# Fourier mixer with folded tokens: two transforms over 256 tokens in place of one over 512

## What is computed

```python
def fourier_mixer(h, w_in, w_out):
    B, N, _ = h.shape
    u, z = jnp.split(h @ w_in, 2, axis=-1)
    ug = u.astype(jnp.float32).reshape(B, N, FT_GROUPS, FT_GROUP_DIM)
    y = jnp.fft.fft2(ug, axes=(1, 3), norm='ortho').real.reshape(B, N, D_INNER)
    return (y.astype(h.dtype) * jax.nn.silu(z)) @ w_out
```

## Time and profile before

| what | value |
|---|---|
| median of 3 runs | 2701.87 us (2699.59 to 2704.38) |
| the profiled execution, its own time | 2705.14 us |
| span from its first to its last instruction | 2703.4 us |
| mean granted TensorE clock | 0.979 |
| TensorE matmul busy | 2556.3 us, 95% of the span |
| DVE busy, ACT busy | 1602.4 us (59%), 1003.5 us (37%) |
| Fourier mixer with its prologue and epilogue | about 1041 to 1315 us of the span |

### The profile page before, as it was taken

How to read it: one execution, slowest core, us unless ns; L and a number is a source line. 1 busy time by engine, 2 the same in 40 slices (tenths; PEclk the granted TensorE clock), 3 DMA queues, 4 the chain that set the end, 5 groups by cost and what they waited for, 6 DMA issues and landing times.

```text
span 2703.4 us, 40281 instructions
## 1 busy us (share of the span) xinstructions
PE 2556.3 (95%) x14516; PEld 2192.1 (81%) x14516; DVE 1602.4 (59%) x2276; ACT 1003.5 (37%) x1334; POOL 113.5 (4%) x140
## 2 busy tenths in 40 slices
PE   6999999999999998999899999989999899999996
PEld 1788888888888775888689999978988667888885
DVE  5567777777777744333455343468999755544445
ACT  3334443443354323333235222235445443322222
POOL 0011211111121000000000000000000000000000
PEclk9999999999999998999899999989999899999998
DMA  5122211222122222211122222222222212222222
GB/s 223 63 70 70 77 63 62 73 75 70 54 78 70 93 94 70 67 65 62 56 86 93 93 85 93 87 84 90 98 86 87 83 56 89 90 95 96 94 93 85
DMA packets 59816, 224.33 MB, mean 83 GB/s; under 512 B 6496, under 2 KB 6496, under 8 KB 59136
## 3 DMA queue, kind: packets, MB, share of 16 engines
q1 hardware_dynamic: 56544, 207.94, 22.8%
q0 software_dynamic: 3232, 15.86, 1.6%
HBM read 221.68 MB, written 2.10 MB: 83 GB/s over the span
## 4 chain that ended last, share of the span: by engine, by line
PE 85%; DVE 7%; ACT 4%; issue 3%; DMA 1%; DVEq 0%; ACTq 0%; SPq 0%; POOL 0%
PE ps L436 74%; PE ps L595 4%; PE ps L617 1%; PE ps L493 1%; DVE w_lo L1310 1%; DVE cv L1870 1%; ACT L934 1%; DMA ada_raw<-in_ada_weights_dram 1%; PE ps L636 1%; PE ps L608 1%; PE ps L627 1%; PE ps L582 1%; PE ps L629 1%; PE ps L628 1%; ACT w_hi L839 0%
## 5 line engine op out<-in xcount | busy, mean ns | idle before, releaser
L839 ACT ACTIVATE w_hi<-w_raw 128x1024 fp32r<-128x1024 f32 x360 | 381.4, 1060 | 1016.2 <-PE ps L436 1010.0
L1310 DVE TENSOR_TENSOR w_lo<-w_raw,w_hi 128x1024 fp32r<-128x1024 f32 x360 | 439.1, 1220 | 281.4 <-ACT w_hi L839 279.5
L436 PE MATMUL ps<-n_hi,w_hi 128*128 128x512 f32 (+1 forms) x992 | 324.0, 358 | 30.1 <-DVE w_lo L1310 16.4
L436 PE MATMUL ps<-n_hi,w_lo 128*128 128x512 f32 (+1 forms) x992 | 320.4, 355 | 0.0
L436 PE MATMUL ps<-n_lo,w_hi 128*128 128x512 f32 (+1 forms) x992 | 320.4, 355 | 0.0
L436 PE MATMUL ps<-h_hi,w_hi 128*128 128x512 f32 x640 | 273.7, 428 | 8.4 <-DVE h_lo L1337 4.4
L436 PE MATMUL ps<-h_hi,w_lo 128*128 128x512 f32 x640 | 255.3, 399 | 0.0
L436 PE MATMUL ps<-h_lo,w_hi 128*128 128x512 f32 x640 | 254.7, 398 | 0.0
L436 PEld LDWEIGHTS ps<-n_hi,w_hi 128*128 128x128 f32 x992 | 175.1, 190 | 66.4 <-issue 21.6
L436 PEld LDWEIGHTS ps<-n_lo,w_hi 128*128 128x128 f32 x992 | 176.3, 191 | 27.2 <-issue 0.2
L436 PEld LDWEIGHTS ps<-n_hi,w_lo 128*128 128x128 f32 x992 | 175.6, 190 | 26.6
(11 more groups left out here) (330 smaller groups left out, 5059.9 us busy)
## 6 DMA issues: line engine op xcount, KB each, us to landing
w_raw<-in_weights_dram SPq DMA_DIRECT2D x376, 512.0 KB, 3.3
ada_raw<-in_ada_weights_dram SPq DMA_DIRECT2D x4, 2048.0 KB, 25.9
gate_raw<-in_gate_weights_dram POOLq DMA_DIRECT2D x16, 512.0 KB, 3.6
x<-in_x_dram SPq DMA_DIRECT2D x1, 2048.0 KB, 11.8
x<-in_x_dram POOLq DMA_DIRECT2D x1, 2048.0 KB, 8.0
out_dram<-fin POOLq DMA_DIRECT2D x1, 2048.0 KB, 6.5
xc<-in_ctx_dram POOLq DMA_DIRECT2D x1, 1024.0 KB, 12.0
F_raw<-in_seq_dft_dram POOLq DMA_DIRECT2D x1, 1024.0 KB, 5.7
```

The source lines that it names most:

```text
L436: last = nc.tensor.matmul(o, w, xp, start=start and n == 0, stop=stop and n == 2)
L839: run(w_hi[:, s], w_raw[:, s], ACT.Copy).then_inc(hi_ready[s], 1)
L1310: tt(w_lo[:, s], w_raw[:, s], w_hi[:, s].bitcast(F32), ALU.subtract).then_inc(lo_ready[s], 1)
```

## The change

Tokens t and 512-t are folded. For t = 1 to 255 the cosine rows of t and 512-t are equal and the sine rows are opposite, so the cosine sums need only u[t] + u[512-t] and the sine sums only u[t] - u[512-t]. Token 0 stands for itself; token 256 is left out of the transform and added behind it as u[256] times +-1/sqrt(512), from a constant row `middle`.

- ACT no longer copies u whole. It copies the upper half of the bank (256 columns) to `u_up`, and DVE's new `fold(k)` writes the sums to `u_st[1:256]`, the differences to `u_st[257:512]` (in0 is PSUM, in1 is `u_up` read backwards) and tokens 0 and 256 to columns 0 and 256.
- `over_tokens(a)` keeps its 12 matmuls, but the six of token tiles 0 and 1 (the sums) run over the 258 first columns of `F` into bank 6 + a, the six of tiles 2 and 3 (the differences) over its 256 last columns into bank 4 + a. `F` holds 256 rows in place of 512.
- `p` is put together from three pieces: DVE adds the middle token to the cosines in `cosines(a)` (128x257, to `p_cos`), ACT copies the sines (128x255, from bank 4 + a) and then `p_cos` to `p_hi`, and DVE makes `p_lo` with two subtractions (`spectrum_lo`). `keep_middle` saves u[256] of both tiles (128x2).
- The semaphore `ft_acc` is parted: banks 0 and 1 are freed for z's projection by the fold (`u_folded`) and for u's by silu(z) (`z_out`).
- The table `F` that is loaded and cut before the loop is half as large; two memsets fill `middle`.

```diff
@@ pe_group
-                    pe.wait_ge(ft_acc, i * 4 + (k + 1))
+                    pe.wait_ge((z_out, u_folded)[k // 2], i * 2 + (k % 2 + 1))
...
-                    pe.wait_ge(ft_acc, j * 4 + 4)
+                    pe.wait_ge(u_folded, j * 2 + 2)
...
                     for t in range(TT):
-                        last = three([ps[:, 6 + a]], u_hi[:, a, tile(t)], u_lo[:, a, tile(t)],
-                                     [F_hi[:, t]], [F_lo[:, t]], t == 0, t == TT - 1)
+                        part, m_ = divmod(t, FOLD)
+                        o, c = ((ps[:, 6 + a, 0:BF], slice(0, BF)),
+                                (ps[:, 4 + a, 0:HALF_T], slice(HALF_T, T)))[part]
+                        last = three([o], u_hi[:, a, tile(t)], u_lo[:, a, tile(t)],
+                                     [F_hi[:, m_, c]], [F_lo[:, m_, c]], m_ == 0, m_ == FOLD - 1)
@@ act_group
+                    if k < 2:
+                        if j is not None:
+                            act.wait_ge(u_folded, i * 2 + (k - 1))
+                        run(u_up[:, k], ps[:, k, HALF_T:T], ACT.Copy).then_inc(up_copied, 1)
+                        return
...
+                def spectrum_hi(a):
+                    if j is not None:
+                        pe(2 + a)
+                        run(p_hi[:, a, HALF_T + 1:T], ps[:, 4 + a, 1:HALF_T], ACT.Copy)
+                        act.wait_ge(cos_done, j * 2 + (a + 1))
+                        run(p_hi[:, a, 0:HALF_T + 1], p_cos[:, a], ACT.Copy).then_inc(act_ft, 1)
...
-                hi(2, p_hi[:, 0], ps[:, 6])
-                hi(3, p_hi[:, 1], ps[:, 7])
+                spectrum_hi(0)
+                spectrum_hi(1)
@@ before dve_group
+            for n in range(2):
+                own.link(v.memset(middle[:, n:HALF_T + 1:2], (-1) ** n / T ** 0.5))
@@ dve_group
+                def fold(k):
...
+                    if j is not None:
+                        dve.wait_ge(pe_ft, j * 5 + 1)
+                    dve.wait_ge(up_copied, i * 2 + (k + 1))
+                    u, up, down = ps[:, k], ps[:, k, 1:HALF_T], u_up[:, k, HALF_T - 1:0:-1]
+                    tt(u_st[:, k, 1:HALF_T], up, down, ALU.add)
+                    tt(u_st[:, k, HALF_T + 1:T], up, down, ALU.subtract)
+                    v.tensor_copy(u_st[:, k, 0:T:HALF_T], u[:, 0:T:HALF_T]).then_inc(u_folded, 1)
...
+                def cosines(a):
...
+                        dve.wait_ge(pe_ft, j * 5 + (2 + a))
+                        stt(p_cos[:, a], middle[:], u_mid[:, a:a + 1], ps[:, 6 + a, 0:HALF_T + 1], ALU.mult, ALU.add
+                            ).then_inc(cos_done, 1)
...
+                def spectrum_lo(a):
...
+                        dve.wait_ge(act_ft, j * 8 + (3 + a))
+                        tt(p_lo[:, a, HALF_T + 1:T], ps[:, 4 + a, 1:HALF_T], p_hi[:, a, HALF_T + 1:T].bitcast(F32),
+                           ALU.subtract)
+                        tt(p_lo[:, a, 0:HALF_T + 1], p_cos[:, a], p_hi[:, a, 0:HALF_T + 1].bitcast(F32), ALU.subtract
+                           ).then_inc(dve_ft, 1)
...
                 next_block(0)
                 lo(1, u_lo[:, 0], ps[:, 4], u_hi[:, 0])
                 lo(2, u_lo[:, 1], ps[:, 5], u_hi[:, 1])
+                keep_middle()
+                fold(0)
                 next_block(1)
-                lo(3, p_lo[:, 0], ps[:, 6], p_hi[:, 0])
-                lo(4, p_lo[:, 1], ps[:, 7], p_hi[:, 1])
+                fold(1)
+                cosines(0)
+                spectrum_lo(0)
+                cosines(1)
+                spectrum_lo(1)
                 next_block(2)
```

More of the change, by code:

```diff
@@ L57 @@
 BF = 258
+HALF_T = T // 2
+FOLD = TT // 2
 _sizes = [("c", 2 * KD), ("ada_b0", 16), ("gate_b", 16), ("ada_b1", 16), ("norm_g0", KD), ("norm_g1", KD),
@@ L228, in program @@
         g_hi, g_lo = f.take("g_hi", [P, KD, T], F32R), f.take("g_lo", [P, KD, T], F32R)
-        F_hi = f.take("F_hi", [P, TT, T], F32R)
-        F_lo = f.take("F_lo", [P, TT, T], F32R)
+        F_hi = f.take("F_hi", [P, FOLD, T], F32R)
+        F_lo = f.take("F_lo", [P, FOLD, T], F32R)
         C_hi = f.take("C_hi", [P, 2, 2, 2, P], F32R)
@@ L240, in program @@
         raw = f.over()
-        F_raw, C_raw = raw.take("F_raw", [P, TT, T]), raw.take("C_raw", [P, 2, 2, 2, P])
+        F_raw, C_raw = raw.take("F_raw", [P, FOLD, T]), raw.take("C_raw", [P, 2, 2, 2, P])
         u_st, zf_st = f.take("u_st", [P, 2, T]), f.take("zf_st", [P, 2, T])
@@ L245, in program @@
         o_sb, yf, yg = f.take("o_sb", [P, 256]), f.take("yf", [P, T]), f.take("yg", [P, T])
+        middle, p_cos = f.take("middle", [P, HALF_T + 1]), f.take("p_cos", [P, 2, HALF_T + 1])
+        u_mid, u_up = f.take("u_mid", [P, 2]), f.take("u_up", [P, 2, HALF_T])
         b = g.over()
@@ L314, in program @@
         meta_scaled, meta_hi = sem("meta_scaled"), sem("meta_hi")
-        ft_acc, pe_ft, act_ft, dve_ft = sem("ft_acc"), sem("pe_ft"), sem("act_ft"), sem("dve_ft")
+        up_copied, u_folded, z_out, cos_done = sem("up_copied"), sem("u_folded"), sem("z_out"), sem("cos_done")
+        pe_ft, act_ft, dve_ft = sem("pe_ft"), sem("act_ft"), sem("dve_ft")
         dft_split = {e: sem(f"dft_split_{e}") for e in ("act", "dve")}
@@ L418, in _ @@
             pool.wait_ge(y_cut, HEADS)
-            pool.dma_start(F_raw[:], dft_in).then_inc(dft_in_s, 16)
+            pool.dma_start(F_raw[:], dft_in[:, 0:FOLD]).then_inc(dft_in_s, 16)
             pool.dma_start(C_raw[:], chan_in).then_inc(chan_in_s, 16)
@@ L872, in square_one @@
                 run(sq, src, ACT.Square).then_inc(R["sq"], 1)
-            for sem_ in (acc_free, ft_acc, mx_acc):
+            for sem_ in (acc_free, z_out, mx_acc):
                 act.sem_inc(sem_, 2)
@@ L1073, in stage @@
                         return
-                    if j is not None:
[L1075 to L1082, removed]
+                    if k < 2:
[3 more added lines that the diff above has]
+                        return
+                    if j is not None:
+                        dve(5 + 2 * (k - 2))
+                    run(zf_st[:, k - 2], ps[:, k % 2], ACT.Silu).then_inc(z_out, 1)
                 def hi(n, dst, src):
@@ L1686, in next_block, with keep_middle @@
                         after(k)
+                def fold(k):
+                    if i is None:
+                        return
+                    if j is not None:
[5 more added lines that the diff above has]
+                    v.tensor_copy(u_st[:, k, 0:T:HALF_T], u[:, 0:T:HALF_T]).then_inc(u_folded, 1)
+                def keep_middle():
+                    if j is not None:
+                        dve.wait_ge(u_folded, j * 2 + 2)
+                        own.link(v.tensor_copy(u_mid[:], u_st[:, :, HALF_T]))
+                def cosines(a):
+                    if j is not None:
+                        dve.wait_ge(pe_ft, j * 5 + (2 + a))
+                        stt(p_cos[:, a], middle[:], u_mid[:, a:a + 1], ps[:, 6 + a, 0:HALF_T + 1], ALU.mult, ALU.add
+                            ).then_inc(cos_done, 1)
+                def spectrum_lo(a):
+                    if j is not None:
+                        dve.wait_ge(act_ft, j * 8 + (3 + a))
[3 more added lines that the diff above has]
+                           ).then_inc(dve_ft, 1)
                 def mirror(m_):
@@ L1693, in mirror @@
                     dve.wait_ge(act_ft, j * 8 + (5 + 2 * m_))
-                    dve.wait_ge(ft_acc, j * 4 + 6)
+                    dve.wait_ge(z_out, j * 2 + 4)
                     tt(yf[:, 1:256], e[:, 1:256], o_sb[:, 1:256], ALU.subtract)
@@ L1719, in _ @@
                 st.enter(j, 4)
-                own.enter(j, 2)
+                own.enter(j, 3)
                 dve_group(j + 1, j)
```

## The result

| what | before | after |
|---|---|---|
| median | 2701.61 us (2699.59 to 2704.38) | 2683.36 us (2679.38 to 2684.97) |
| profiled execution, its own time | 2705.14 us | 2684.97 us |
| span, mean granted clock | 2703.4 us, 0.979 | 2683.3 us, 0.978 |
| DVE busy, ACT busy | 1602.4 us, 1003.5 us | 1622.8 us, 1002.2 us |

The ratio after to before is 0.9927, with a 95% interval of 0.9913 to 0.9941. The forecast was 2680.7 us in a range of 2677 to 2688; faster was right.

The account below looks back on a forecast made before the run. The prediction took TensorE alone to bound the loop, at 31.59 us a pass. Loop 18.2, prologue 0.5 and group 7 2.5 us sum to 21.2 us off the 2701.87 us median: 2680.7 us, range 2677 to 2688.

Parts of the forecast that it names:

- TensorE's term: In the loop, over_tokens' 24 matmuls fall from 5.47 to 2.87 us: 2.60 us a pass, 18.2 us in seven passes.
- The first rival: Weight loads pace the short F matmuls at 188 ns, saving only 0.04 us each: about 2692 us; chance 4%.
- The added work: In the loop, DVE gets some 2.9 us more a pass, covered; the chain to over_channels(0) keeps 1.7 us of slack.
- The second rival: The p chain ahead of over_channels(0) exceeds its slack by less than 2.6 us; at 1 us a pass, 2688 us; 7%.
- The prologue: Before the loop, the halved table removes TensorE's wait ahead of project(2): gain 0.5 us, between 0 and 0.5.
- Group 7: After the loop, shorter F matmuls, partly at half clock, bring over_channels(0) forward from 1306.63 to 1304.1 us: 2.5 us.
- a late return: In group 7, if full clock returns only behind the shorter F burst, over_tokens(1) ends at 1302.7 and 1.9 us remain.

Follow-up runs that it names:

- the delayed kernels: Changed kernel with three or six chained 128x512 memsets on DVE between fold(1) and cosines(0): 2681.32 us with three, 2703.98 us with six.
- the later ones: The changed kernel measured again, unaltered, twice on other chips, against the kernel before: 2681.7 us (ratio 0.9919) and 2681.24 us (0.9918).
- spare matmuls: Changed kernel with matmuls that nobody reads filling TensorE's four gaps in group 7: 2675.74 us, ratio to the kernel before 0.9900.
- the loosened wait: Changed kernel, group 7's transposes no longer waiting for group 6's last y_lo: 2680.78 us, ratio 0.9910; with spare matmuls too, 2675.45 us, 0.9895.

## Why the prediction was right, point by point

**TensorE's term** was 2.60 us a pass and 18.2 us in all; measured 2.59 and 18.17. It came from taking the price of a short matmul from a row of the same shape, same order of loads and same loop (over_channels), and not from halving 0.228 us (0.114, which would have made 19.2 us in seven passes). F's matmuls ran at 0.120 us, each with its load (median 192 ns now). The first rival, loads that pace them at 188 ns, fell with this, and with it the quoted rule of the Trainium skill's page "TensorE: Matmul & The Clock Gate" as a measure of this stream: it allowed under 50 ns a matmul, the runs show 108 (0.228 and 0.120 us).

**The added work.** Prices by row: fold(1) 0.83 us laid out, 0.82 to the end of its last copy in the trace and 0.73 to the start of cosines(0); the backward read costs nothing (0.42 us, as forward); cosines 0.47 for 0.45, ACT's copy of p_cos 0.42 for 0.40 to 0.44. The chain ended 1.73 us ahead of its reader, laid out at 1.7, and the delayed kernels gave 1.72 and 1.70 us from outside. The second rival had its place right, but no time was missing there. DVE's busy time in the whole rose by 20.4 us, and none of it was paid in the loop.

**The prologue** gave 0.59 us, forecast 0.5 as the most: TensorE's wait ahead of project(2) is gone (0.49 us from the first matmul to project(2)), and with it the slower first matmul behind the wait (1057.55 to 1057.89, 0.34 us in place of 0.23).

**Group 7** is the term that was mis-sized: 2.5 us forecast, 1.42 measured. The step that failed is the clock's return. I had put it at the moment at which it had come in the trace of before, some 4 us after the first F matmul. In the changed kernel all 24 F matmuls ran at half clock (5.28 us from the first to the end of the last, laid out as 4.7), so from the first F matmul to over_channels(0) it is 7.39 us in place of 9.24: 1.85 us less where 2.5 was to be seen, and what I had worked out for a late return (1.9 us). That bound missed the transposes, which ran at half clock to the end, 1.94 us for 1.49, and put the first F matmul 0.45 us later. My reading that group 7 had started at half clock before was wrong there: between 1294.40 and 1295.00 the granted clock was still 0.91, and then 0.50.

When the clock rises moves between executions. With the same instructions on TensorE up to there, it came back 5.2 to 5.8 us after the first F matmul in three traces of the changed kernel, and some 15 matmuls or 3.1 to 3.3 us after it in those with three and six memsets. One trace of it is a draw, not a duration.

**The total.** 21.2 us forecast, 20.1 by the traces, 18.3 by the first medians, 21.0 and 21.7 by the later ones. The first median, 2683.36 us, is 2.7 us above the forecast: 1.1 us of that is group 7, the rest is within the spread of single times. That the later medians come within 0.5 us of 21.2 is no proof of the term that was wrong. The spread has a place: the stretch ahead of the mixer ended at 1041.16 and 1041.07 us in the first two traces, and between 1035.29 and 1040.37 in the other traces of kernels that are the same up to there. From the first projection matmul to the residual the changed kernel took 253.56, 253.67 and 253.51 us.

## What to carry to other kernels

When one engine is busy without a gap, price what you take from it by a row of the shape that it will have, then lay out the longest chain that runs beside it to its reader, instruction by instruction: the slack so found was right to 0.05 us, and it says how much may be added for nothing. Where the gain of a change falls into a stretch with idle TensorE, give its clock a range. And look at such stretches for spare matmuls: here four lots of them, without effect on any result, gave 2.97 us ahead of the residual and 1.5 us in it by the traces, and with the loosened wait 5.8 us by the times, beside the 20.1 us of the transform.

## What was not expected of the hardware

A gap of 2.07 us on TensorE let the granted clock fall in two of six equal passes and left it at full in four. Ahead of over_channels(0) in group 7, gaps of 1.50 us (the kernel before) and 1.91 us (the changed kernel) were followed by matmuls at full clock. In two of the changed kernel's three traces it then fell within over_channels: distances of 0.12 us turn to 0.21 us at 1288.07 in the first, in over_channels(1), and at 1284.93 in the second, near the end of over_channels(0). But a gap of 1.97 us at the same place, in the run with three memsets, was followed by 16 matmuls at half clock:

```profile
1282.37 0.41 PE L442 MATMUL ps<-p_hi,C_hi 128*128 128x258 f32 x1 [1.97 <-DVE p_lo L1738]
1282.59 0.42 PE L442 MATMUL ps<-p_lo,C_hi 128*128 128x258 f32 x1
```

No run here separates what decides it. Behind the gaps of 4.0 to 5.2 us in these traces the matmuls ran at half clock from the first or second on. The one exception is the transposes of group 7 in the kernel before, where the clock fell some 0.5 us after they had begun.
